# The last 16 value rows of retention, and the 16 gate columns of the even layer, multiplied from unsplit numbers in four column groups

## The reference, cut to what matters

```
q, k, v, g = columns of h @ w_in                 # (272, 4 x 128) each
s = (q_rope @ k_rope.T) * decay                  # token i sees tokens j up to the end of its chunk of 64
o = s @ v                                        # then normalised per head over its 128 features, gated
```

```
g_low = y @ w_in[:, 3072:3088]                   # (256, 16), y is h after its norm
log_a = log_sigmoid(g_low @ w_gate_up + b) / 16  # (256, 4 x 64)
```

## Time and profile before

| | |
|---|---|
| median of three runs | 1790.46 us (1790.15 to 1790.73) |
| the profiled execution, its own time | 1793.75 us |
| its span (first to last instruction) | 1791.9 us |
| mean granted clock of TensorE | 0.979 |
| TensorE (PE) busy | 1713.9 us, 96% |
| VectorE (DVE) busy | 1172.3 us, 65% |
| ScalarE (ACT) busy | 817.4 us, 46% |
| GpSimd (POOL) busy | 237.6 us, 13% |

### The profile page before, as it was taken

The page is one execution under the profiler, slowest core; times in us unless marked ns, Lnnn a source line. Parts: engine busy times, 40 slices in busy tenths (PEclk is TensorE's granted clock), DMA queues, the critical chain, the costliest instruction groups (busy, mean ns, idle before and its releaser), DMA issues.

```text
span 1791.9 us, 32601 instructions
## 1 busy us (share of the span) xinstructions
PE 1713.9 (96%) x13384; PEld 1662.4 (93%) x13384; DVE 1172.3 (65%) x1594; ACT 817.4 (46%) x1062; POOL 237.6 (13%) x212
## 2 busy tenths in 40 slices
PE   7999999999999999999999996999899999889998
PEld 6999999899999999998899995998899998889997
DVE  5556597685566755587686544566866568677664
ACT  5333373563435433364564433564533345354333
POOL 0002400310032000500230042231100020020000
PEclk9999999999999999999999998998999999999998
DMA  5545443344544445442355552332445533144552
GB/s 208 170 181 185 167 150 118 118 165 167 196 172 150 176 172 204 148 174 97 127 194 188 204 194 95 115 133 95 165 177 192 194 141 106 50 143 184 187 204 78
DMA packets 37864, 281.52 MB, mean 157 GB/s; under 512 B 4384, under 2 KB 4512, under 8 KB 7184
## 3 DMA queue, kind: packets, MB, share of 16 engines
q1 hardware_dynamic: 36016, 271.73, 42.3%
q0 software_dynamic: 1760, 8.56, 1.4%
HBM read 279.23 MB, written 1.05 MB: 156 GB/s over the span
## 4 chain that ended last, share of the span: by engine, by line
PE 76%; DVE 10%; ACT 7%; issue 3%; DMA 2%; POOL 1%; SPq 0%; ACTq 0%; DVEq 0%; POOLq 0%
PE bank L682 24%; PE bank L684 23%; PE bank L683 23%; DVE w_lo L2045 4%; ACT w_hi L1422 4%; DMA raw<-in_up_w 1%; ACT h L1486 1%; ACT h_hi L1485 1%; PE bank L1035 1%; POOL h L618 1%; PE bank L1060 0%; PE bank L987 0%; PE bank L703 0%; PE bank L1220 0%; DVE h L2212 0%
## 5 line engine op out<-in xcount | busy, mean ns | idle before, releaser
L2045 DVE TENSOR_TENSOR w_lo<-raw,w_hi 128x2048 fp32r<-128x2048 f32 (+3 forms) x239 | 580.6, 2429 | 277.8 <-ACT w_hi L1422 277.5
L682 PE MATMUL bank<-h_hi,w_hi 128*128 128x272 f32 (+1 forms) x2336 | 673.4, 288 | 21.2 <-DVE h_lo L2201 10.0
L684 PE MATMUL bank<-h_hi,w_lo 128*128 128x272 f32 (+1 forms) x2336 | 669.4, 287 | 0.0
L683 PE MATMUL bank<-h_lo,w_hi 128*128 128x272 f32 (+1 forms) x2336 | 668.1, 286 | 0.0
L1422 ACT ACTIVATE w_hi<-raw 128x2048 fp32r<-128x2048 f32 (+2 forms) x242 | 481.5, 1990 | 316.5 <-PE bank L684 311.7
L682 PEld LDWEIGHTS bank<-h_hi,w_hi 128*128 128x128 f32 x2336 | 444.3, 190 | 27.9 <-issue 16.3
L684 PEld LDWEIGHTS bank<-h_hi,w_lo 128*128 128x128 f32 x2336 | 444.3, 190 | 0.0
L683 PEld LDWEIGHTS bank<-h_lo,w_hi 128*128 128x128 f32 x2336 | 443.5, 190 | 0.1
L682 PE MATMUL bank<-g_hi,w_hi 128*128 128x256 f32 (+1 forms) x1344 | 386.8, 288 | 13.8 <-DVE y L2253 4.0
L684 PE MATMUL bank<-g_hi,w_lo 128*128 128x256 f32 (+1 forms) x1344 | 382.6, 285 | 0.0
L683 PE MATMUL bank<-g_lo,w_hi 128*128 128x256 f32 (+1 forms) x1344 | 381.7, 284 | 0.0
(11 more groups left out here) (363 smaller groups left out, 1863.3 us busy)
## 6 DMA issues: line engine op xcount, KB each, us to landing
raw<-in_up_w SPq DMA_DIRECT2D x131, 1024.0 KB, 4.8
raw<-in_down_w SPq DMA_DIRECT2D x48, 1408.0 KB, 5.9
raw<-in_in_w SPq DMA_DIRECT2D x20, 1024.0 KB, 4.9
raw<-in_out_w SPq DMA_DIRECT2D x16, 1024.0 KB, 4.9
raw<-in_even_w SPq DMA_DIRECT2D x12, 1024.0 KB, 4.9
raw<-in_odd_w SPq DMA_DIRECT2D x6, 1024.0 KB, 4.8
diag<-in_conv_w POOLq DMA_DIRECT2D x4, 1024.0 KB, 5.1
raw<-in_in_w SPq DMA_DIRECT2D x4, 512.0 KB, 3.5
```

Of the source, the lines that this page charges most:

```text
L682: pe.matmul(out, w[0], x[0], start=first, stop=False)
L683: pe.matmul(out, w[0], x[1], start=False, stop=False)
L684: return pe.matmul(out, w[1], x[0], start=False, stop=last)
L2045: last = dve.tensor_tensor(lo[:, b:n], raw[:, slot, b:n], hi[:, b:n].bitcast(F32), ALU.subtract)
```

## The change

The last 16 tokens' values and the gate tile are no longer made of 24 matmuls of split numbers. They are 8 plain fp32 matmuls, one for each block of 128 features, with a stationary operand 32 wide (the last 32 tokens, or 32 weight columns) taken from `h` or `raw` themselves. Feature block k goes to the 32 output partitions of group k mod 4, so that PSUM holds four partial sums one above the other. Nothing adds them: what multiplies with them next sums over all 128 partitions. For retention that needs the last 32 tokens' keys four times side by side (`k_tail`, two new DVE copies into `conv_sq`), decay factors four times (zero for the 16 tokens that are not the last), and 128 rows in place of 16 in the scores, the decay and the values. For the gate it needs `gup` four times.

`raw` is now read by PE. Its slot is given back by a new semaphore, `raw_used`: the loads of chunks 9 and 10 in each layer, and of chunk 5 in the even layer, wait for it too. The two DVE copies stand in step 6, after the rope and ahead of the taps, behind a wait for the rope's last result; PE's scores wait for them.

```diff
+            def k_tail(j):
+                return conv_sq[:, j, 0:2 * P]
...
-            def straight(chunks):
+            def straight(chunks, raw_use=lambda i: 0):
                 for i, (src, blocks) in enumerate(chunks):
+                    if raw_use(i):
+                        sp.wait_ge(raw_used, raw_use(i))
                     load(src, blocks, i)
...
+            def last_tokens(bank, slot):
+                for half in range(2):
+                    for g in range(4):
+                        k = 4 * half + g
+                        last = pe.matmul(bank[TAIL * g:TAIL * (g + 1), 0:2 * P], h[:, k, T - TAIL:],
+                                         raw[:, slot, 2 * k * P:(2 * k + 2) * P], start=half == 0, stop=half == 1)
+                last.then_inc(raw_used, 1)
+
+            def gate_tile(bank, slot, tiles, e):
+                for half in range(2):
+                    for g in range(4):
+                        k = 4 * half + g
+                        col = (k * tiles + e) * P
+                        last = pe.matmul(bank[TAIL * g:TAIL * (g + 1), 0:S], raw[:, slot, col:col + TAIL], y[:, k, 0:S],
+                                         start=half == 0, stop=half == 1)
+                return last
...
                     if order[z] in by_token:
                         for e in range(2):
                             bank_is_free(z + e)
+                        if len(tokens) > 2:
+                            last_tokens(bank(z + 1), st.slot(c))
                         for t, m in enumerate(tokens):
+                            if m < P:
+                                continue
...
                     for hd in range(HEADS):
-                        last = pe.matmul(ps[7][0:m, hd * n:(hd + 1) * n], kT[:, hd, lo:lo + m],
+                        last = pe.matmul(ps[7][:, hd * n:(hd + 1) * n], k_tail(hd // 2)[:, hd % 2 * P:(hd % 2 + 1) * P],
                                          qT[:, hd, SEEN_FROM[2]:], start=True, stop=True)
...
-                    for t, (lo, m) in enumerate(KTOK):
-                        last = pe.matmul(ps[VALUE_BANKS[hd]][:, SEEN_FROM[t]:T], v_tok[0:m, t, hd * P:(hd + 1) * P],
-                                         pT[0:m, hd, SEEN_AT[t]:SEEN_AT[t] + T - SEEN_FROM[t]],
+                    for t in range(3):
+                        last = pe.matmul(ps[VALUE_BANKS[hd]][:, SEEN_FROM[t]:T], v_tok[:, t, hd * P:(hd + 1) * P],
+                                         pT[:, hd, SEEN_AT[t]:SEEN_AT[t] + T - SEEN_FROM[t]],
                                          start=t == 0, stop=t == 2)
...
-                        last = pe.matmul(ps[3][:, j * S:(j + 1) * S], gup[0:16, j, :], gb[0:16, :],
+                        last = pe.matmul(ps[3][:, j * S:(j + 1) * S], gup[:, j, :], gb[:],
...
+                    if c == 6:
+                        dve.wait_ge(rope_ready, l * (2 * HEADS + 1) + 2 * HEADS)
+                        for j in range(2):
+                            keys = kT[:, 2 * j:2 * j + 2, T - TAIL:].rearrange("p h (a n) -> p h a n", a=1)
+                            last = dve.tensor_copy(k_tail(j).rearrange("p (h a n) -> p h a n", h=2, n=TAIL),
+                                                   keys.broadcast_to([P, 2, TAIL_COPIES, TAIL]))
+                        last.then_inc(rope_ready, 1)
```

More of the change, by code:

```diff
@@ L967, in in_tiles @@
                                                    wpair(slot, 2 * k, 2), k == 0, k == KD - 1)
+                            elif order is EVEN_ORDER and order[z] == GATE_TILE:
+                                last = gate_tile(bank(z), st.slot(c), tiles, e)
                             else:
@@ L971, in in_tiles @@
                                                k == 0, k == KD - 1)
-                            last.then_inc(chunk_used if e == tiles - 1 else tile_ready, 1)
+                            last.then_inc(raw_used if order is EVEN_ORDER and order[z] == GATE_TILE else
+                                          chunk_used if e == tiles - 1 else tile_ready, 1)
                             z += 1
@@ L1660, in in_tiles @@
                     for e in range(tiles):
-                        tile_is_ready(c, e, tiles)
+                        if order is EVEN_ORDER and order[z] == GATE_TILE:
+                            act.wait_ge(raw_used, 2 * LAYERS + 1)
+                        else:
+                            tile_is_ready(c, e, tiles)
                         copy(order[z], bank(z))
@@ L1742, in copy @@
                         else:
-                            m = KTOK[2][1]
-                            last = act.activation(v_tok[0:m, 2, i * P:(i + 2) * P], bank[0:m, 0:2 * P], ACT.Copy)
+                            last = act.activation(v_tok[:, 2, i * P:(i + 2) * P], bank[:, 0:2 * P], ACT.Copy)
                     else:
@@ L1877, in copy @@
                 else:
-                    last = act.activation(gb[0:16, :], bank[0:16, 0:S], ACT.Copy)
+                    last = act.activation(gb[:], bank[:, 0:S], ACT.Copy)
                 last.then_inc(z2_copied, 1)
@@ L2515, in decayed_tails @@
                     dve.wait_ge(ret_s, seen.next(ret_s))
-                    m, o = KTOK[2][1], SEEN_AT[2]
-                    dve.tensor_tensor(pT[0:m, :, o:], ps[7][0:m, 0:HEADS * (SEEN - o)].rearrange("p (h n) -> p h n", h=HEADS),
-                                      decay[0:m, :, o:], ALU.mult).then_inc(ret_p, 1)
+                    o = SEEN_AT[2]
+                    dve.tensor_tensor(pT[:, :, o:], ps[7][:, 0:HEADS * (SEEN - o)].rearrange("p (h n) -> p h n", h=HEADS),
+                                      decay[:, :, o:], ALU.mult).then_inc(ret_p, 1)
                 def centred(g):
                     dve.wait_ge(z_copied, seen.at(z_copied, 16 + 2 * g))
-                    m = KTOK[2][1]
-                    two = v_tok[:, 0:2, 2 * g * P:2 * (g + 1) * P].rearrange("p t (h n) -> p t h n", n=P)
-                    tail = v_tok[0:m, 2, 2 * g * P:2 * (g + 1) * P].rearrange("p (h n) -> p h n", n=P)
-                    dve.tensor_reduce(v_sum[:, g], two, AX.X, ALU.add)
-                    dve.tensor_reduce(v_sum2[0:m, g], tail, AX.X, ALU.add).then_inc(v_summed, 1)
+                    three = v_tok[:, :, 2 * g * P:2 * (g + 1) * P].rearrange("p t (h n) -> p t h n", n=P)
+                    dve.tensor_reduce(v_sum[:, g], three, AX.X, ALU.add).then_inc(v_summed, 1)
                     dve.wait_ge(v_summed, seen.next(v_summed))
-                    for t in range(2):
+                    for t in range(3):
                         rows = v_tok[:, t, 2 * g * P:2 * (g + 1) * P].rearrange("p (h n) -> p h n", n=P)
                         sums = v_sum[:, g, t, :].rearrange("p (h n) -> p h n", n=1).broadcast_to([P, 2, P])
-                        dve.scalar_tensor_tensor(rows, sums, -1.0 / P, rows, ALU.mult, ALU.add)
-                    sums = v_sum2[0:m, g, :].rearrange("p (h n) -> p h n", n=1).broadcast_to([m, 2, P])
-                    dve.scalar_tensor_tensor(tail, sums, -1.0 / P, tail, ALU.mult, ALU.add).then_inc(v_cent, 1)
+                        last = dve.scalar_tensor_tensor(rows, sums, -1.0 / P, rows, ALU.mult, ALU.add)
+                    last.then_inc(v_cent, 1)
                 def conv_centred():
@@ L2938, in tables @@
         n = T - SEEN_FROM[i]
-        dk[0:m, :, SEEN_AT[i]:SEEN_AT[i] + n] = d[:, lo:lo + m, SEEN_FROM[i]:].transpose(1, 0, 2)
+        for at in range(0, P, TAIL if m < P else P):
+            at += (TAIL - m) % TAIL
+            dk[at:at + m, :, SEEN_AT[i]:SEEN_AT[i] + n] = d[:, lo:lo + m, SEEN_FROM[i]:].transpose(1, 0, 2)
     t["decay"] = dk
@@ L3090, in lay_out @@
     gup = np.zeros((P, 2, P), np.float32)
-    gup[0:16] = i["gla_w_gate_up_2"][0].reshape(16, 2, P)
+    for at in range(0, P, TAIL):
+        gup[at:at + 16] = i["gla_w_gate_up_2"][0].reshape(16, 2, P)
     a["gup"] = gup
```

20 lines of the change are left out of this document (12 added, 8 removed).

## The result

The changed kernel takes **1782.8 us** (median of five runs; 1790.5 before, measured beside it). The ratio is 0.9944, 95% interval 0.993 to 0.9959: faster by 0.56%. Forecast were 1782.2 us, within 1778.5 to 1788. The profiled execution has a span of 1781.0 us and a time of its own of 1782.83.

A forecast was written before the change was run, and what follows sets the result against it. PE's own queue was taken to bound the kernel (busy 96% of the span). Gains of 2 x (0.55 + 1.5 + 1.25) + 1.75 = 8.35, say 8.3 us, off 1790.5 gave 1782.2 us, range 1778.5 to 1788.

The forecast's parts named there:

- The burst: Eight fp32 matmuls in chunks 7, 8 and the even layer: four column groups run side by side, 1.2 us a burst.
- rival 1: The four column groups line up: a burst takes 3.7 us, the kernel 1792.8 us (1800.3 with extra stalls); chance 0.09.
- A: Chunk 7, in each of two layers: PE saves 1.5 us but waits for DVE, gain 0.55 us a layer.
- PE would wait for DVE: At line 1084, behind chunk 7, PE's idle time grows from 0.33 to over 1 us, released by DVE.
- B: Chunk 8, in each of two layers: a burst replaces 24 matmuls, gain 1.5 us a layer.
- C: Heads' outputs, two layers: changes of form into and out of 16 rows go, gain 1.25 us a layer.
- D: Even layer, once: a burst replaces the gate tile's 24 matmuls, gain 1.75 us (bounds 0.9 to 2.1).
- rival 2: A held load takes 8.5 us and lands late (chunks 9, 5): 1784.6 us; 0.14 together with the third rival.
- I found no such wait: In chunks 8 to 12 and the whole even projection, PE meets no wait like that for DVE's last convolution sum.
- The held loads: Chunks 9 to 11 and the even layer's chunk 5 load later at zero cost; cover 1.8, over 3, 2.5 us.
- Rivals 2 and 3: The third: C's or B's gain is given back at a wait behind, 1784.6 us; 0.14 together with rival 2.
- The sum: Two layers and the even layer: 2 x (0.55 + 1.5 + 1.25) + 1.75 = 8.35 us; forecast's chance 0.74.

The follow-up runs named there:

- Experiment 4: Changed kernel with the value burst unpacked (stationary of 128 tokens, no column groups), gate tile left packed: 1790.0 us, ratio 0.999 to the kernel before.
- 10: Changed kernel with the retention burst's loops swapped, both matmuls of a column group behind one another: one run, 1780.9 us.
- experiment 8: Changed kernel with the third matmul of each head's output at 16 rows again: 1786.2 us, ratio 0.9957 to the kernel before.
- experiment 12: Kernel before with DVE's reciprocal ahead of the logits, nothing else: one run, 1793.4 us; chunk 3 to the scores unchanged at 66.82 us.
- Experiment 3: Changed kernel with DVE's reciprocal ahead of the next unit's logits: 1782.0 us, ratio 0.9964 to the kernel before.
- experiment 5: Changed kernel again, unedited, beside the kernel before: 1781.1 us against 1793.2, ratio 0.994.
- 6: Changed kernel with the key copies on ACT and the reciprocal ahead of the logits: 1782.1 us, ratio 0.9945 to the kernel before.
- 7: Changed kernel with key copies on ACT, reciprocal ahead of the logits and the convolution's mean behind chunk 8's first token group: 1781.2 us, ratio 0.9938.
- 11: Changed kernel with key copies on ACT and the convolution's mean behind chunk 8's first token group, reciprocal left behind the logits: 1781.5 us, ratio 0.9939.

## Why the prediction was right

**The burst.** Forecast 1.2 us, measured 1.0. Line 1147 of the earlier trace rows was the right row to argue from: overlap of column groups carries over from two to four. The first four records start 7 ns apart. Experiments 4 and 10 show that the packing carries it, in either order of the loops. The rule of the Trainium skill (page "TensorE: Matmul & The Clock Gate", Part 3, "The mechanism"), that a weight load overlaps matmuls in flight only where its row group differs, doesn't hold here: 16 loads that share all rows start within 0.5 us in the changed kernel. The prediction made too much of that one sentence: a table of the same Part ("Measured speedup vs the span model") lists three column groups side by side at 2.38 times the speed, and the trace agrees with the table: four groups take 1.0 us for what takes 3.3 one behind another. Experiment 4 built what rival 1 feared for the values, a burst of 3.3 us one matmul behind another (the gate tile stayed packed), and came out at no change.

**A** was 0.84 instead of 0.55 us because the copies cost 0.5 and not 0.8 us: a copy of 128x256 numbers from SBUF is a record of 0.29 us, the two together 0.50, and not the 0.42 each of the copy from PSUM in the earlier trace rows. That is the lower bound of the copies that the prediction gave (0.85 gained). The row had the right size and the wrong source. That PE would wait for DVE was right, but for less: 0.8 us, not over 1.

**B and C** came within 0.11 us (1.61, 1.32). That C hangs on the 16 rows is shown by experiment 8; the prediction's split of it wasn't met. It had the changes of form alone as the reason, and 0.11 us for each narrow record of 128 rows. In the trace the second of these starts 0.056 us behind the first, and the first 272-column record behind them takes 0.285 us in place of 0.23, so that a head costs 1.0 us all the same.

**D was the term that failed:** 0.65 us for 1.75. I had checked whether a load (rival 2) would be late and not what PE asks of POOL. The earlier trace rows show ACT, DVE and PE there and no row of POOL, so the cover of POOL's first division wasn't worked out. "I found no such wait" was true of the trace before, and there the cover was 0.6 us (experiment 12). Counted from chunk 3, PE came to the division 1.8 us sooner and then stood 1.3 us. Experiment 3 takes the wait away and gives 2.04, more than forecast, in part since the burst costs 1.0 and not 1.2 us.

**The held loads** cost nothing. The load of chunk 9 was issued at 276.96 and that of the even layer's chunk 5 at 1135.69; ACT waited 1.6 us for the latter, and PE never did. Rivals 2 and 3 didn't come about.

**The sum** of the stages was 8.2 for 8.35. It is right partly because two errors cancel: the layers gave 0.9 us more together, the even layer 1.1 less. The median lies within the sum's own range, 1779.6 to 1786.7, without the 1.5 us that the prediction allows for the clock; between the two profiles that allowance was too small, as 2.7 us lie outside the stages. The medians differ by 7.6 us in the first comparison and by 12.1 in experiment 5's, so the whole time says no more than 8 to 12 us, and that the forecast lies 0.6 us from the first median is in part luck.

**What stays open** is why the kernel before meets longer half-rate stretches at three norms. It has one of 6.8 us at two or three of them in each of its three profiles; of the eleven profiles with the change or parts of it, nine have none and two have one. That the change shifts the work against the clock's own pace is my guess; no run moved the work alone.

**No variant is shown to beat the changed kernel.** Experiments 6, 7 and 11 take 0.4 to 2.4 us out of the stages, and their ratios (0.9945, 0.9938, 0.9939) can't be told from 0.994.

## What to carry to other kernels

Matmuls that use only 16 or 32 stationary columns can share the array in column groups, at about the time of the records of one group; look for a row with two groups and argue from it. Where PE is made faster ahead of a wait, list all that PE asks for next, from every engine, with the time each has in hand: the queue that I left out (POOL) was the one that decided. A gain of about 1 us ahead of a half-rate stretch may come back as a longer one (experiments 3, 6 and 7), so read such gains by stages and don't expect them in the whole time.

## What the hardware showed that I had not expected

- POOL's division of 2 x 128x128 took 1.2 us alone and 3.2 to 3.6 us beside DVE's split of 2.27 us, that of 2 x 128x256 1.8 and 3.4 to 3.6 us; in experiment 3, with no split beside them, all eight took 1.2 to 1.9. This agrees with the Trainium skill (page "SBUF — State Buffer", "Who interferes with whom"), which has an instruction of VectorE with two inputs in SBUF hold up one of GpSimd that reads SBUF. Which of them starts first matters in the trace as well: in the kernel before, the POOL instruction that began at 1150.31, 0.15 us ahead of a split, took its usual 0.93 us (the split took 2.47), and the next, begun at 1151.21 beside that split, took 2.51.
- Fewer rows cost more here: the four heads took 5.26 us with 16-row tails between records of 128 rows and 3.94 with 128-row tails, so 0.16 us less for each of the 8 tail records.
- The stretch at 1.2 GHz behind the even layer lasted 20.5 us in place of 17.1 in all three profiles in which the scores ahead of it came 1.4 us sooner after chunk 3.
